# One block of engine programs for input projection and attention, on overlaid buffers

## The reference

```
h = rms_norm(x, norm_mix);  proj = h @ w_in            # 3072 columns: q k v | B C u
q, k = rms_norm per head;   8 heads of 64
z = q.k / 8, s < t only;    a = sigmoid(z_ts) * prod_{s<j<t} (1 - sigmoid(z_tj));   attn = a @ v
conv = B * conv_w3(C * u)                              # causal, width 3, 512 channels
x = x + concat(attn, conv) @ w_out
x = x + (silu(h2 @ w_gate) * (h2 @ w_up)) @ w_down,    h2 = rms_norm(x, norm_ffn)
```

## Time and profile before

| | us |
|---|---|
| median of 3 runs | 2661.18 (2660.74 to 2662.26) |
| the profiled execution | 2662.36 |
| its span, first instruction to last | 2660.5 |
| PE busy | 2518.8 (95%) |
| DVE / ACT / POOL busy | 1303.8 / 1139.8 / 1239.7 |
| mean granted TensorE clock | 0.981 of full speed |

### The profile page before, as it was taken

One profiled execution on the slowest core, in us unless ns is written; L12 is line 12 of the kernel. 1 busy time (PEld: TensorE's weight loads), 2 busy tenths in 40 slices (PEclk: granted clock), 3 DMA queues, 4 the chain that ended last, 5 costly groups with the idle time before them and its releaser, 6 DMA issues.

```text
span 2660.5 us, 34870 instructions
## 1 busy us (share of the span) xinstructions
PE 2518.8 (95%) x12272; PEld 2082.3 (78%) x12272; DVE 1303.8 (49%) x1315; ACT 1139.8 (43%) x1857; POOL 1239.7 (47%) x865
## 2 busy tenths in 40 slices
PE   8999879999899999799799999999999999999999
PEld 6788657777777777678678888888887888888887
DVE  4433346776676677534564544432534545442222
ACT  3222256766676677432343333322433333332322
POOL 1212156767667676301375544423486455442332
PEclk9999989999999999899899999999999999999999
DMA  5665573343533522254422122256543222214554
GB/s 174 192 186 158 159 195 98 109 131 99 145 90 94 157 73 66 89 166 143 158 80 94 60 83 95 94 165 207 190 145 101 95 71 79 87 63 154 166 190 154
DMA packets 299865, 336.03 MB, mean 126 GB/s; under 512 B 17888, under 2 KB 239072, under 8 KB 298720
## 3 DMA queue, kind: packets, MB, share of 16 engines
q1 hardware_dynamic: 299744, 334.57, 41.0%
HBM read 240.13 MB, written 94.37 MB: 126 GB/s over the span
## 4 chain that ended last, share of the span: by engine, by line
PE 48%; POOL 1%; DMA 1%; DVE 0%; ACT 0%; issue 0%; SPq 0%; ACTq 0%; DVEq 0%
PE ffn_ps L1791 10%; PE ffn_ps L1793 10%; PE ffn_ps L1795 10%; PE ffn_ps L76 6%; PE ffn_ps L77 6%; PE ffn_ps L78 6%; POOL ffn_A L1731 1%; DMA ffn_raw<-in_w_up 1%; ACT ffn_A L1461 0%; DVE ffn_raw L1601 0%; DVE ffn_raw L1611 0%; DVE ffn_raw L1606 0%; DVE ffn_s L1647 0%; DVE ffn_s L1597 0%; ACT ffn_s L1473 0%
## 5 line engine op out<-in xcount | busy, mean ns | idle before, releaser
L1731 POOL TENSOR_TENSOR ffn_A<-ffn_raw,ffn_A 128x512 fp32r<-128x512 f32 x264 | 364.7, 1392 | 379.0 <-ACT ffn_A L1461 378.7
L1791 PE MATMUL ffn_ps<-all_B,ffn_A 128*128 128x512 f32 x1232 | 481.3, 391 | 17.9 <-POOL ffn_A L1731 15.8
L1793 PE MATMUL ffn_ps<-all_B,ffn_A 128*128 128x512 f32 x1232 | 480.7, 390 | 0.0
L1795 PE MATMUL ffn_ps<-all_B,ffn_A 128*128 128x512 f32 x1232 | 480.6, 390 | 0.0
L829 DVE TENSOR_TENSOR_SCAN att_stick<-att_z,att_stick 128x128 f32<-128x128 f32 (+5 forms) x192 | 331.2, 1726 | 221.8 <-ACT att_z L741 210.5
L875 POOL TENSOR_TENSOR att_a<-att_a,att_stick 128x128 f32<-128x128 f32 (+5 forms) x192 | 281.6, 1472 | 215.3 <-DVE att_stick L829 214.5
L1736 POOL TENSOR_TENSOR ffn_A<-ffn_A_over,ffn_A 128x512 fp32r<-128x512 f32 x88 | 160.3, 1821 | 333.7 <-ACT ffn_A L1494 333.7
L1791 PEld LDWEIGHTS ffn_ps<-all_B,ffn_A 128*128 128x128 f32 x1232 | 232.3, 189 | 67.4 <-POOL ffn_A L1731 19.1
L1639 DVE TENSOR_TENSOR ffn_A<-ffn_A_over,ffn_A 128x1024 fp32r<-128x1024 f32 x88 | 117.3, 1333 | 322.2 <-ACT ffn_A L1492 322.2
L76 PE MATMUL ffn_ps<-ffn_A 128*128 128x512 f32 x704 | 273.9, 389 | 0.0
L77 PE MATMUL ffn_ps<-ffn_A 128*128 128x512 f32 x704 | 273.9, 389 | 0.0
(11 more groups left out here) (122 smaller groups left out, 5035.7 us busy)
## 6 DMA issues: line engine op xcount, KB each, us to landing
ffn_A_over<-in_w_down SPq DMA_DIRECT2D x88, 512.0 KB, 3.5
att_w_stage<-in_w_in SPq DMA_DIRECT2D x48, 512.0 KB, 4.4
ffn_raw<-in_w_gate SPq DMA_DIRECT2D x22, 1024.0 KB, 6.7
ffn_raw<-in_w_up SPq DMA_DIRECT2D x22, 1024.0 KB, 8.8
hidT<-ffn_s SPq DMA_DIRECT2D x88, 256.0 KB, 2.4
ffn_A_over<-hidT SPq DMA_DIRECT2D x88, 256.0 KB, 3.7
qkv_x_t<-in_x SPq DMA_DIRECT2D x16, 512.0 KB, 4.5
hT_hi<-qkv_hT_hi SPq DMA_DIRECT2D x16, 512.0 KB, 5.4
```

Source lines behind the costliest of these rows:

```text
L1731: nc.gpsimd.tensor_tensor(A[:, j, p, 1, :, :], operand(j, p), A[:, j, p, 0, :, :].bitcast(F32), ALU.subtract).then_inc(lo_done, 1)
L1791: nc.tensor.matmul(ps[:, b, :], A[:, j, p, 0, k, :], B[p][:, 0, k, :], start=first_mm, stop=False, skip_group_check=True)
L1793: nc.tensor.matmul(ps[:, b, :], A[:, j, p, 0, k, :], B[p][:, 1, k, :], start=False, stop=False, skip_group_check=True)
L1795: mm = nc.tensor.matmul(ps[:, b, :], A[:, j, p, 1, k, :], B[p][:, 0, k, :], start=False, stop=last_mm, skip_group_check=True)
```

## The change

`project_attend_stage` allots all tiles of both stages by hand and runs one block. `qkv_stage` and `attend_conv_stage` give back programs as functions; attention's program of each engine calls the projection's first, and hands it things to do early (`Ahead`).

SBUF: the conv weight tiles, taps and halo have places of their own; attention's queries lie over the projection's `w_stage`, keys over gain, x and square, conv rows, V and `a` over `w_hi` (blocks n = 0, 1, 2), conv rows lo and aT_hi over `w_lo`, stick and the conv's tiles over xn and hT, aT_lo over qk_n, v_out and qkT. For that the projection's weights are kept as [P, 3, KT, 512] instead of [P, KT, 1536]. PSUM is one tile of 8 banks: the projection takes 0 to 5 for proj, 6 and 7 for its transposes; attention z in 0, 1 and 4, 5, transposes in 2, 3, proj in 6, o in 7.

```diff
+            def load_taps(sp): ...           # in projection step 0, ahead of its hT stores
+            def load_ahead(sp):              # in projection step 14, ahead of its hT stores
+                load_w(0, 0)
+                load_w(0, 1)
+                sp.wait_ge(opening.qkT_stored[0], 2 * DMA * (SAFE // 2 + 1))
+                sp.wait_ge(opening.qkT_stored[1], 2 * DMA * (SAFE // 2))
+                sp.wait_ge(opening.xn_done, TILES)
+                sp.wait_ge(opening.ss_done, TILES)
+                load_k(0, 0)                 # SAFE = 13 token tiles of it
+                load_q(0, 0)
+                load_q(0, 1)
+            def load_rows(sp):               # in step 15, behind store_qk(14), ahead of the v store
+                sp.wait_ge(opening.proj_full, 3 * (TILES - 1) + 1)
+                for i in range(KT):
+                    load_hT(0, i)
+            def start_up():
+                for b in range(2):
+                    sp.wait_ge(opening.v_stored[b], DMA * TILES // 2)
+                    sp.wait_ge(opening.qkT_stored[b], DMA * TILES)
+                    sp.wait_ge(opening.hT_stored[b], DMA * TILES)
+                load_v(0, 0)
+                load_k_rest()                # the last 3 tiles of keys of head 0
+            opening.programs.sync(sp, Ahead(load_taps, load_ahead, load_rows))
```

The waits of SP for all stores at the end of the projection's block are gone. On ACT and POOL `w_split(0, 0)` is done at the end of projection step 14 (their `tiles` now have tail=3). The transposes of tile 15 become `rest`:

```diff
 PE    scores(p, n)
+                    if is_first(p) and n == 0:
+                        rest(0)
+                        rest(1)
+      in scores: at n == 1 wait for qk_n_done, v_done; at h == 0 and t == SAFE for k_rest
 ACT   sigmoids(p, n)
+                    if is_first(p) and n == 0:
+                        rest()
+      in take: before the first c_sb, wait for qk_ss_done and hT_stored
 DVE
+            for b in range(2):
+                dve.wait_ge(opening.hT_stored[b], DMA * TILES)       # ahead of stick's memset
       running_product(p, n)
+                    if is_first(p) and n == 0:
+                        rest()
+                    if is_first(p) and n == LAG:                     # LAG = 3; ahead of aT_part(0)
+                        for b in range(2):
+                            dve.wait_ge(opening.v_stored[b], DMA * TILES // 2)
+                            dve.wait_ge(opening.qkT_stored[b], DMA * TILES)
```

More of the change, by code:

```diff
@@ L108, in _, with run @@
             dve.wait_ge(copied, 2)
-def qkv_stage(nc, cst, x, norm_mix, w_in, q_norm, k_norm, hT_hi_dram, hT_lo_dram, qk_hi_dram, qk_lo_dram, v_dram):
+@dataclass
+class Programs:
+    sync: object
+    gpsimd: object
+    scalar: object
+    vector: object
+    tensor: object
+def run(nc, programs):
+    with nc.Block() as block:
+        @block.sync
+        def _(sp):
+            programs.sync(sp)
+        @block.gpsimd
+        def _(pool):
+            programs.gpsimd(pool)
+        @block.scalar
+        def _(act):
+            programs.scalar(act)
+        @block.vector
+        def _(dve):
+            programs.vector(dve)
+        @block.tensor
+        def _(pe):
+            programs.tensor(pe)
@@ L194, in step @@
                     load_x(t + 2, b)
+                if first:
+                    att.load_taps(sp)
+                if isinstance(t, int) and t == TILES - 2:
+                    att.load_ahead(sp)
                 sp.wait_ge(hT_lo_done, NB * t + NB)
@@ L212, in _, with gpsimd @@
             store_qk(TILES - 1, (TILES - 1) % 2)
[L213 to L219, removed]
+        def gpsimd(pool, att):
             def x_rstd(t, b):
@@ L240, in step, with scalar @@
                                         ALU.pow).then_inc(qk_rstd_done, 1)
-            tiles(pool, step)
-        @block.scalar
-        def _(act):
+                if isinstance(t, int) and t == TILES - 2:
+                    att.pool_ahead(pool)
+            tiles(pool, step, tail=3)
+        def scalar(act, att):
             def x_square(t, b):
@@ L309, in step, with rest, vector @@
                         hT_part(2, 0, n)
[L311 to L316, removed]
+            tiles(act, step, tail=3)
+            def rest():
+                for n in range(2):
+                    qkT_part(TILES - 1, (TILES - 1) % 2, n)
+            return rest
+        def vector(dve, att):
             def x_norm(t, b):
@@ L394, in _, with rest, tensor @@
             tiles(dve, step)
[L395 to L399, removed]
+            def rest():
+                for n in range(2):
+                    qkT_part(TILES - 1, (TILES - 1) % 2, n)
+            return rest
+        def tensor(pe, att):
             def x_transpose(t, b, n):
@@ L528, in attend_conv_stage @@
     head_end = [group_units[HG], NU]
[L530 to L555, removed]
@@ L558, in key_slot @@
+    plan = plan()
     def key_slot(n):
```

351 lines of the change are left out of this document (223 added, 128 removed).

## The result

The changed kernel takes 2643.72 us (median of 4 runs, 2642.3 to 2644.45), against 2660.96 us of the kernel before beside it (4 runs, 2660.5 to 2662.26). The ratio is 0.9936, 95% interval 0.9921 to 0.9951. The forecast was 2644.1. The profiled execution took 2644.42 us with a span of 2642.6, 17.9 us less than before.

The account below looks back on a forecast made before the run. PE is busy 95% of the span, but loads pace the seam from 319 to 373 us. One term, 17.1 us there, off the 2661.2 us median gives 2644.1 us; other parts zero; range 2636.5 to 2651.5.

Parts of the forecast that it names:

- First score right behind the last projection matmul: At the seam, early loads let PE start scores at 319.0 instead of 337.3 us, shrinking the seam by 18.3 us here.
- rival D: The change fails: PE's first score waits for something in the new order, seam as before, 2660 us; chance 0.03.
- The tail between two units: Projection's tail between attention's first units: both qkT stores ready at 325.2 instead of 323.4; ACT ready for weight tile 2 about 346.
- The new wait is the queue in front of weight tile 2: Rows, stores and nine issues delay this load; it lands at 352.3, ACT waits about 6 us, gain 17.1 us.
- The rows: The 16 hT row loads of step 15, 4.19 MB, drain at 374 GB/s in 11.2 us, to 331.8.
- Rival B: Rows share engines with stores and drain at 229 GB/s, 18.3 us; gain only 10.0 us, 2651.2 us; chance 0.13.
- Taps moved to step 0: Conv taps issued from 34.97 us, ahead of tile 0's hT stores: zero cost, at most 1.5 us late.
- Refusal 0 to 2.4 us, taken 1.2: Behind the long V load, the queue may refuse an issue before weight tile 2; ends 0 and 2.4 us, middle taken.
- Places: New SBUF and PSUM places of weights, scores and attention's tiles: zero, since instructions of one shape cost the same across banks.
- Each event kept 17 us earlier from there: After ACT's split of weight tile 2, units, queue order and plan are unchanged, so the 17 us won is kept.
- A: Stores pass the rows or the queue is quicker; weight tile 2 not waited for, gain 23.7 us, 2637.5 us; chance 0.17.
- C: Attention's 192 units each cost 0.12 us more from alternating banks, 23 us against 17, so 2667 us; chance 0.05.

Follow-up runs that it names:

- the form alone: Kernel before with only the projection's weights kept as three blocks [P, 3, KT, 512], tiles at their old places: 2661.44 us beside 2660.6, ratio 1.0002.

## Why the prediction was right, and where it was lucky

The time was met within 0.4 us, and that is luck: the forecast is one term, 17.1 us from the seam. The seam gave 12.2 us in one trace and 13.8 in the other. What filled the gap is a term that the forecast put at nothing, the places of the tiles.

- **First score right behind the last projection matmul: right.** 15.41 us of idle PE are gone. There is no new wait for keys, so rival D is out.
- **The tail between two units: right in kind, small in price.** The second transposes waited 3.20 us instead of 1.66. ACT was ready at 340.3, which is 28.2 us behind its copy of the last v; the forecast had 346 - 319.1 = 26.9.
- **The new wait is the queue in front of weight tile 2: right, and mis-sized in three terms.** I count from the copy of v. V's load came 332.92 - 312.11 = 20.8 us behind it, forecast 337.5 - 319.07 = 18.4: 2.4 us late. The nine issues took 6.5 us, forecast 6.8. The tile took 10.9 us to land, forecast 8.0: 2.9 us late. That is 5.0 us, and the seam gave 12.2 instead of 17.1. In the second trace V's load came 21.1 us behind the copy, but the tile landed 9.0 us after its issue. So the price of this load is 9 to 11 us, near the high end of the earlier trace rows. The low end was misread: tile 0, with 6.0 us, did not have "little ahead" but two loads of keys and four of queries, issued from 329.00 to 332.11; what it did not have ahead were the rows, V and the taps. The four issues of query groups 2 and 3 stand in front of tile 2, and moving these away brought the split 2.4 us forward, counted from the copy of v (34.1 us against 36.5).
- **The rows do not drain at 374 GB/s.** They were issued over 11.6 us (309.79 to 321.4), with single issues of up to 1.65 us. The last store of tile 14 landed at 314.5 and the last row at 328.5: 14.0 us for the 4.19 MB, where the forecast had 11.2. The stores behind made up for a part: the last one landed 4.3 us behind the last row, forecast 5.2. That stores land behind rows issued ahead of them is right: 10.3 us after issue, against 4.6 in the earlier trace rows. Rival B's mechanism is partly true (2.8 of its 7.1 us).
- **Taps moved to step 0: zero, right.** 2.03 us, not 8.64. **Refusal 0 to 2.4 us, taken 1.2:** K's first issue took 1.52 us, 0.9 more than its neighbours. With the rows behind the stores it was 5.93 us; that the wait for the stores had emptied the queue first is the likely reason.
- **Step 14: zero, right.** **The plan: zero**, nothing shows against it.
- **Places: zero, wrong.** This is the step of the prediction that failed. The earlier trace rows compares DVE's instructions on PSUM banks; no row was read that says anything of SBUF addresses under PE. In the projection it was worth 4.1 to 4.4 us by the traces of the kernels told above, and 4.0 and 5.1 us by the medians of the two kernels that have the aligned places and nothing else. The rest of the 7 us is chance of the two traces. The first matmul of tile 2 starts at 50.87 instead of 51.76, but at 51.98 in the second trace of the changed kernel, and between 51.1 and 52.8 in the others. And the granted clock in 70 to 84 us is 0.76 instead of 0.63, but it is 0.76 in all traces except those of the kernel before and of the form alone.
- **Each event kept 17 us earlier from there: nearly.** The 2 us given back in attention may have a cause in the same finding. Conv products read hT_hi (moving) and w_hi (stationary). Before, they lay 200992 - 160032 = 40960 bytes apart, 80 times 512; now 71008 - 25856 = 45152, which is 96 over a multiple of 512, as in the kernel with the weights moved.

The groups of conv matmuls of the kernel before, 394 to 1079 us (mean ns in the middle):

```profile
L78 PE MATMUL att_proj<-att_hT_hi,att_w_lo 128*128 128x512 f32 x353 | 138.9, 393 | 0.0
L77 PE MATMUL att_proj<-att_hT_lo,att_w_hi 128*128 128x512 f32 x353 | 137.9, 391 | 0.0
```

The same of the changed kernel, 375 to 1060 us:

```profile
L104 PE MATMUL lay_ps<-lay_hT_hi,lay_w_lo 128*128 128x512 f32 x352 | 139.3, 396 | 0.0
L103 PE MATMUL lay_ps<-lay_hT_lo,lay_w_hi 128*128 128x512 f32 x352 | 139.3, 396 | 0.0
```

From start to start, three conv matmuls in a row take 0.722 to 0.723 us in the kernel before and in the seven made from it, and 0.733 in both traces of the changed kernel and in the four made from it. Times the 384 such groups that is 3.8 us. This was read from traces; no kernel with the conv weights moved was run. The total does not prove it: from the split of weight tile 2 to the last transposes it is 732.0 us before and 734.4 after, but the eight traces with the old attention have 731.6 to 734.5, and the six with the new one 732.7 to 736.4. The clock behind the hole differs by some tenths too. Slices of the kernel before:

```profile
373.00:377.00 4.00, 3.91 (x21) 3.94 (x22) 3.37 (x3) 2.16 (x4) 1.06 (x2) 0.59 1.13 333
377.00:381.00 4.00, 3.96 (x26) 3.00 (x24) 1.87 (x4) 2.83 (x7) 1.67 (x1) 1.00 0.21 39
```

And of the changed kernel:

```profile
354.00:358.00 4.00, 4.00 (x19) 4.00 (x20) 3.37 (x4) 2.01 (x4) 1.07 (x2) 0.50 1.11 305
358.00:362.00 4.00, 4.00 (x27) 3.47 (x26) 1.17 (x2) 2.28 (x5) 1.51 (x1) 0.91 0.29 62
```

At 0.50, the level of 1.2 GHz, and 0.91 against 0.59 and 1.00, PE gets (0.09 + 0.09) x 4 = 0.7 us less of its full clock. How long this low spell lasts differs among traces of either kernel, so this is no price of the change.

- **Rivals.** A, weight tile 2 not waited for, did not happen by itself; the kernel that loads it ahead makes it true and gives 2639.1, where A had 2637.5. C, slower scores, is out in its mechanism (banks): the last transposes come 730.8 us behind the hole, against 728.4, which is 0.013 us a unit where C needed 0.09 (729.0 us in the second trace); but the conv products do show a price of places in attention.

The balance of the profiled spans: 7.0 (projection) + 12.2 (seam) - 2.1 (given back until the output projection) = 17.1, and 17.9 over the whole span.

## What to carry to other kernels

When tiles move, compute the distance in bytes between the two operands of every long run of matmuls, before and after; one unused tile won 2% of the pace of this one. A distance 128 bytes over a multiple of 512 was enough to lose it. Where loads are moved ahead of a seam, list the queue up to the load that ends the last wait, and move that load too: here a few lines more were worth 7.7 us, where the whole change had brought 17. A long issue in the timeline of a queue belongs to what is under way in front of it, and passes for the most part to whatever stands there next. And before a difference of 1 or 2 us between two traces is explained, read it in a second trace of the same kernel.

## What the runs showed of the hardware

- Three 128x512 products of rounded float32, with the clock at 1.00, follow each other in 0.689 to 0.690 us when the moving and the stationary operand lie a multiple of 512 bytes apart in a partition, in 0.705 us when they lie 128 bytes over one, and in 0.708 to 0.709 us at 96 and 416. Why, and whether a multiple of 256 would be enough, was not tried.
- A DMA issue takes 0.4 to 0.6 us in most places; the same ones, behind a backlog, took up to 7.25 us (the query load), and the four of the taps 2.03 us without and 8.64 with one.
- The low-clock spell near 72 us lasted 10.2 us in 2 and 6.8 us in 12 of 14 traces, and not by layout. The longer one cost the projection 1.5 us more (266.9 against 265.4 us).
- A copy between the Sigmoid work costs no table load: one load of 1.28 us at 312.72, and none at the copies and sigmoids that alternate up to 351 us.
